# Products of the identity in PE's waits: two and four at a norm, ten at the double norm, twenty in the routing

## The chip, the cores and the metric

The kernel runs on one core of one Trainium2 chip. The metric is the device time of one execution, in microseconds, as the median of several runs. Everything is computed in float32. TensorE (PE in the rows) multiplies, VectorE (DVE) and ScalarE (ACT) do the elementwise work, SyncE (SP) issues nearly all weight loads, and GpSimd (POOL) makes a few copies.

## What is computed

One sequence of 256 tokens, 1024 channels, goes through a first block of two layers (RWKV-7 and latent attention beside each other, then a dense feed-forward layer in layer 0, a mixture of eight experts in layer 1) and a second block of two hybrid attention layers with feed-forward layers. Every half of a layer begins with an RMS norm:

```
def rmsnorm(x, g):
    y = x * rsqrt(mean(x * x, axis=-1, keepdims=True) + eps)
    return y * g

# first block, layers l = 0, 1
h = rmsnorm(x, norm_mix[l]) * (1 + scale) + shift        # "n1"
x = x + gate * (merged @ w_o[l])
h = rmsnorm(x, norm_ffn[l]) * (1 + scale) + shift        # "n2"
f = swiglu(h, ...) if l == 0 else moe_swiglu(h, ...)      # the experts: logits, top 2 of 8, softmax
x = x + gate * f
# between the blocks: rmsnorm(x, norm_final) is "nf", and the norm after it "m1" of layer 0
# second block, layers l = 0, 1
h = rms_norm(x, attn_norm[l])                             # "m1"
h = rms_norm(x, ffn_norm[l])                              # "m2"
x = x + (silu(gate) * up) @ w_ffn_out
```

## The kernel before

Activations lie transposed, channels on the 128 partitions and the 256 tokens along the free side, in eight tiles of 128 x 256. PE's program is written out by hand in one order (`def _(pe)`), and so are the programs of the other engines; semaphores are the only tie between them. Every product goes through the helper `mm` at L524, so nearly all PE rows carry that line. One float32 product is two records of the trace (one transpose is one record).

**Banks.** PE writes into four banks in rotation. `take(key)` gives the next bank and waits until its last reader has released it (`drained`); `take_upper` and `take_beside` do the same for other areas, which the rows call accum. Each call of `take` therefore moves all later uses of the rotation by one bank.

**A norm** has these steps on PE: sums over the channels, by products with one moving column (`zeroed_columns`, then `column_sums`, 12 records where single, 24 otherwise); then ACT takes the root of two columns and DVE the reciprocal, for which PE waits (`inverted`); then `norm_rows` spreads the result over 128 partitions with two products of 128 columns (four records, out<-con,ncol); then DVE multiplies x by it, tile after tile (at n1 and n2 ACT adds a shift to each), and PE waits for the first tile (`h_ready`) before the first product of the next projection. `norm_sums` is called for n2 of both layers, n1 of layer 1, m2 of both layers, and m1 of layer 1; `two_norm_sums` does m1 of layer 0 and nf together, after the experts. The very first norm uses neither.

**The routing** is the start of `experts`. PE turns h to natural order (four times four transposes, L880), with the logits' transposition between the first and the second; then comes a small product for lambda; then PE waits until DVE has picked the two experts of each token (`selected`), and counts positions (`pos`, ten records of 8 columns). From these DVE works out which expert stands at which place (`place_ids`, L2185); SP waits for that before it issues the first expert weights (L2808). DVE goes on to build selection matrices (`grouped`); PE waits for them and gathers the tokens with products of 480 columns (`static`). Then come 168 pieces of expert weights of 2 MB each, in five buffers.

Of the kernel before, what the change touches and what calls it, by code (L numbers as in the profile page):

```python
# [27 lines left out]
P = 128  # L28
# [194 lines left out]
def build(nc, A, out):  # L223
    ctx = ExitStack()
    with ctx:
# [9 lines left out]
        con = sb("con", [P, NCONST])  # L235
# [120 lines left out]
        def reader_of(key):  # L356

            return drained[used_banks[key][0]]
# [25 lines left out]
        ident, blk = c("ident"), c("blk")  # L384
# [132 lines left out]
        def _(pe):  # L517
# [4 lines left out]
            def mm(o, lhsT, rhs, start=True, stop=True, last=False, skip=False):  # L522

                ins = nc.tensor.matmul(o, lhsT, rhs, start=start, stop=stop, skip_group_check=skip)  # L524
                if wide_release and not last:
                    ins.then_inc(wide_used[wide_release.pop(0)], 1)
                elif release and not last:
                    ins.then_inc(ring_used[release.pop(0)], 1)
                return ins

            def take(key):

                b, k, per = used_banks[key] = banks.next()
                if k or per:
                    pe.wait_ge(drained[b], count(k, per))
                return bank[b], filled[b]
# [75 lines left out]
            def attention(tag, q_of, k_of, v_of, rows, take_scores, beside=None):  # L612
# [23 lines left out]
                for hd in range(n):  # L636
# [8 lines left out]
                    if beside:  # L645
# [6 lines left out]
                    mm(t[rows(hd), P:T], v_of(hd, 1), pT[:, hd % 2, T:T + P], False, True, last=True,  # L652
                       skip=True).then_inc(f, 1)

            def first_norm_sums(tag):

                place = []

                def pair(p):
                    if p == 0:  # L660
                        place.extend(take(tag + (0,)))
                    t, f = place
                    pe.wait_ge(x_squared, next_of("x_squared"))
                    for k in (2 * p, 2 * p + 1):
                        ins = mm(t[:, 0:T], ones[:, :], sq[:, k, :], k == 0, k == KD - 1, last=k == KD - 1)
                    if p == 3:
                        ins.then_inc(f, 1)

                return pair

            def zeroed_columns(key, take=take):

                t, f = take(key)
                mm(t[:, 0:TT], zeros, con[:, 0:TT], True, False, skip=True)
                return t, f
# [6 lines left out]

            def norm_rows(key, at, take=take):

                pe.wait_ge(inverted, next_of("inverted"))
                t, f = take(key + ("rows",))
                for a in range(TT):
                    ins = mm(t[:, a * P:(a + 1) * P], ncol[:, at + a:at + a + 1].to_broadcast([P, P]), ident, last=True)
                ins.then_inc(f, 1)

            def norm_sums(tag, take=take, single=False):

                def pair(p):
                    if p < 3:
                        return
                    t, f = zeroed_columns(tag + (0,), take)
                    one_ = ones[:, 0:1]
                    if single:
                        pe.wait_ge(squares_added, next_of("squares_added"))
                        column_sums(t, 0, sq, one_)  # L700
                        pe.wait_ge(x_squared, next_of("x_squared", 4))
                        column_sums(t, 6, sq, one_)
                        pe.wait_ge(x_squared, next_of("x_squared"))
                    else:
                        pe.wait_ge(squares_added, next_of("squares_added"))
                        column_sums(t, 0, sq, one_)
                        column_sums(t, 1, sq, one_)
                        pe.wait_ge(x_squared, next_of("x_squared", 3))
                        column_sums(t, 4, sq, one_)
                        column_sums(t, 5, sq, one_)  # L710
                        pe.wait_ge(x_squared, next_of("x_squared"))
                        column_sums(t, 6, sq, one_)
                    column_sums(t, 7, sq, one_, True).then_inc(f, 1)
                    norm_rows(tag, 2, take)

                return pair

            def two_norm_sums():

                def pair(p):  # L720
                    if p < 3:
                        return
                    (t0, f0), (t1, f1) = zeroed_columns(("nf", 0)), zeroed_columns(("m1", 0, 0))
                    pe.wait_ge(x_squared, next_of("x_squared", 8))
                    for k in (6, 7, 0):
                        if k == 0:
                            pe.wait_ge(squares_added, next_of("squares_added"))
                        column_sums(t1, k, sq, c("eps", 0, 1))
                        ins = column_sums(t1, k, sqg, ones[:, 0:1], k == 0)
                    ins.then_inc(f1, 1)  # L730
                    for k in (6, 7, 0):
                        ins = column_sums(t0, k, sq, ones[:, 0:1], k == 0)
                    ins.then_inc(f0, 1)
                    norm_rows(("m1", 0), 2)
                    norm_rows(("nf",), 6)

                return pair
# [136 lines left out]
            def experts(norm):  # L874

                for a in range(TT):
                    for g in range(2):
                        t, f = take(("hnat", a, g))
                        for i in range(4):
                            ins = nc.tensor.transpose(t[:, i * P:(i + 1) * P], h[:, g * 4 + i, a * P:(a + 1) * P], ident)  # L880
                        ins.then_inc(f, 1)
                        if a == g == 0:
                            pe.wait_ge(*read_out(("logit_parts",)))
                            t, f = take(("logits",))
                            for b in range(TT):
                                ins = mm(t[:, 8 * b:8 * b + 8], logit_parts[:, b * P:(b + 1) * P], c("pick_q", 0, 8), last=True)
                            ins.then_inc(f, 1)
                pe.wait_ge(lam_prod, next_of("lam_prod"))
                t, f = take(("lam",))
                mm(t[:, 0:4], ones[0:64, :], small[0:64, 0:4], last=True).then_inc(f, 1)  # L890
                pe.wait_ge(selected, next_of("selected"))
                t, f = take(("pos",))
# [3 lines left out]
                mm(t[:, 16:24], ones[:, :], router["sel"](0), True, False, last=True)  # L896
                mm(t[:, 16:24], ones[:, :], router["sel"](1), False, True, last=True).then_inc(f, 1)
                pe.wait_ge(*read_out(("hnat", 1, 1)))
                pe.wait_ge(grouped, next_of("grouped"))
                for k in range(KD):  # L900
                    t, f = take(("static", k))
# [27 lines left out]
                for n, (kind, i, k) in enumerate(PIECES):  # L929
                    first, last = (k == 0, k == KD - 1) if kind != "d" else (k % 4 == 0, k % 4 == 3)  # L930
# [6 lines left out]
                    for j in range(NJ):  # L937
                        key = ("e" + kind, i, j) if kind != "d" else ("ed", i, k // 4, j)
# [8 lines left out]
                        for c4 in range(4):  # L947
# [5 lines left out]
                            ins = mm(o[r, 0:WAYS], tokens, weights(n, s), first, last, last=last and c4 == 3, skip=True)  # L953
# [14 lines left out]
                for m in range(KD):  # L968
# [3 lines left out]
                    ins = combine(m)  # L972
# [8 lines left out]
            t, f = take(("c",))  # L981
# [5 lines left out]
            for k in range(0, KD, 2):  # L987
                t, f = take(("xT", k))
                for i in range(2):
                    for a in range(TT):  # L990
                        ins = nc.tensor.transpose(t[:, i * T + a * P:i * T + a * P + P],
                                                  x_nat[:, a, (k + i) * P:(k + i + 1) * P], ident)
# [20 lines left out]
            for l in range(2):  # L1013
# [38 lines left out]
                i = 0  # L1052
                for _, n, ms in B1_PIECES:
                    s, w = piece(8, n)
                    for lo, M, at in ms:
                        t, f = take(("in", l, at))
# [98 lines left out]
                for ch in range(NCH):  # L1155
# [4 lines left out]
                    for name in ("X", "Y"):  # L1160
                        ts = [take((name, l, ch, par)) for par in range(2)]
                        for j in range(RJ):
                            for par, (t, f) in enumerate(ts):
                                r = slice(64 * par, 64 * par + 64)
                                if name == "X":
                                    ins = mm(t[rc, j * 64:j * 64 + 64], AT[r, j, tc], state[r, j, :], last=True)
                                else:
                                    ins = mm(t[r, j * 64:j * 64 + 64], state[r, j, :], RT[r, j, tc], last=True)
# [4 lines left out]
                    t, f = take(("U", l, ch))  # L1173
                    for hd in range(HEADS):
                        ins = mm(t[rc, hd * 64:hd * 64 + 64], Tt4[a][rc, (hd % 2) * 4 + hd // 2, :],
                                 xrhs[rc, hd * 64:hd * 64 + 64], last=True)
# [3 lines left out]
                    t, f = take(("S", l, ch))  # L1180
                    for hd in range(HEADS):
# [4 lines left out]
                        ins = mm(o, Kn[rc, a, hc], Vn[rc, a, hc], False, True, last=True, skip=True)  # L1186
# [6 lines left out]
                for a in range(TT):  # L1193
                    ts = [take(("yl", l, 2 * a + cp)) for cp in range(2)]
                    for hd in range(HEADS):
# [3 lines left out]
                        i = (hd % 2) * 4 + hd // 2  # L1199
                        for cp, rc in halves:  # L1200
                            mm(ts[cp][0][r, at], U[rc, a, hc], RB4[a][rc, i, :], True, False, last=True, skip=True)
                        for cp, rc in halves:
                            ins = mm(ts[cp][0][r, at], Vn[rc, a, hc], RK4[a][rc, i, :], False, True, last=True, skip=True)
# [30 lines left out]
                t, f = take(("krot", l))  # L1234
                mm(t[0:96, 0:T], c("rot96")[0:96, :], qa[0:96, 5, :], last=True).then_inc(f, 1)
                s, w = piece(2)
                for i in range(4):
                    t, f = take(("kn_", l, i))
                    for k in range(2):
                        for half in range(2):  # L1240
                            at = (2 * i + half) * P
                            ins = mm(t[64 * half:64 * half + 64, 0:T], w(k, at, at + 64), qa[:, 3 + k, :], k == 0, k == 1,
                                     last=k == 1, skip=True)
                    ins.then_inc(f, 1)
                for a in range(TT):
                    t, f = take(("vn_", l, a))
# [27 lines left out]
                else:  # L1274
                    pe.wait_ge(router_in, next_of("router_in", 32))
                    t, f = take(("logit_parts",))
                    for k in range(KD):
                        r = slice(STRIP * (k % 4), STRIP * (k % 4 + 1))
                        ins = mm(t[r, 0:T], rt[:, k * STRIP:(k + 1) * STRIP], normed_h(k), k < 4, k >= 4, last=True, skip=True)
# [5 lines left out]
            for l in range(2):  # L1285
# [68 lines left out]
                for _, n, kind in B2_PIECES:  # L1354
# [3 lines left out]
                    if kind == "nat":  # L1358
                        for a in range(TT):
                            t, f = take(("nat", l, nat, a))  # L1360
# [7 lines left out]
                    elif kind == "idx":  # L1368

                        t, f = take(("tr", l, 10))  # L1370
                        for k in range(KD):
                            for half in range(2):
                                ins = mm(t[64 * half:64 * half + 64, 0:T], w(k, 0, 64), h[:, k, :], k == 0, k == KD - 1,
                                         last=k == KD - 1, skip=True)
# [3 lines left out]
                        for a in range(TT):  # L1378
                            t, f = take(("iw", l, a))
# [1520 lines left out]
```

## Time and profile before

| | |
|---|---|
| median of 3 runs | 2949.95 us (2945.87 to 2951.54) |
| the profiled execution, its own time | 2941.82 us |
| its span, first to last instruction | 2940.2 us |
| mean granted TensorE clock | 0.984 |
| PE, ACT, DVE busy | 2833.6, 489.0, 722.7 us |
| DMA | 634.18 MB, mean 216 GB/s |

Read it so: PE is busy nearly all the time, so what counts is how long PE's own work takes and what it waits for. The granted clock is TensorE's share of full speed: 1.00 is 2.4 GHz and 0.50 is 1.2 GHz. A mean of 0.984 says that it stood at the lower level for some 3% of the span. A matmul's busy time is longer than its share of the pace, since matmuls overlap: the pace is read from the time that a row of several records takes.

### The profile page before, as it was taken

The page shows a single profiled execution, that of the slowest core. Times are in us where ns is not written, and L with a number is a line of the kernel's source. Part 1 is how long each engine was busy: PE and PEld are TensorE (multiplying, and loading weights), DVE is VectorE, ACT ScalarE, POOL GpSimd, SP SyncE. Part 2 cuts the span into 40 slices and gives each one's busy share as a digit, 9 for nine tenths or more (in the row PEclk, how much of TensorE's full clock was granted, in tenths as well). Part 3 has the DMA queues.
Part 4 walks back from the last instruction along what each step waited for, and adds up shares of the span by engine and source line. Part 5 has one row for each costly group of instructions (what it writes and reads, how often), then busy time and mean ns, then how long its engine had stood idle before and what let it go on. Part 6 is the DMA issues. An engine that isn't in the chain of part 4 may idle for free.

```text
span 2940.2 us, 49988 instructions
## 1 busy us (share of the span) xinstructions
PE 2833.6 (96%) x20416; PEld 1872.1 (64%) x20416; DVE 722.7 (25%) x1713; ACT 489.0 (17%) x1007; POOL 233.2 (8%) x410
## 2 busy tenths in 40 slices
PE   7999999999988999999999999999999999999999
PEld 5777788887867432322222222277888888878888
DVE  4422454434243101011101101135520002632000
ACT  3213210032232100000000000014420003350000
POOL 4000000000000122222222121200000000000000
PEclk9999999999998999999999999999999999999999
DMA  9562378732220999999999999933343434333442
GB/s 299 163 196 95 101 252 275 259 111 81 67 86 29 353 362 374 375 378 372 378 371 378 370 385 368 362 117 120 115 138 120 166 125 140 120 113 123 150 159 85
DMA packets 435572, 634.18 MB, mean 216 GB/s; under 512 B 29802, under 2 KB 244992, under 8 KB 435216
## 3 DMA queue, kind: packets, MB, share of 16 engines
q1 hardware_dynamic: 406544, 600.97, 59.1%
q10 hardware_dynamic: 26400, 28.76, 3.0%
q8 instruction: 162, 2.65, 0.4%
q0 software_dynamic: 2400, 1.26, 0.2%
q14 instruction: 66, 0.54, 0.1%
HBM read 629.82 MB, written 1.05 MB: 215 GB/s over the span
## 4 chain that ended last, share of the span: by engine, by line
PE 67%; SPq 23%; issue 6%; DVE 2%; ACT 1%; DMA 1%; ACTq 0%; DVEq 0%
PE bank L524 47%; SPq L2808 20%; PE accum L524 19%; SPq L2794 2%; DVE w L1920 1%; SPq L2735 1%; PE bank L643 1%; DMA ring<-in_ada_w_dram 0%; ACT L1430 0%; DMA ring<-in_moe_w_dram 0%; PE bank L1084 0%; ACT sh L1430 0%; PE bank L880 0%; DVE h L1926 0%; ACT h L1430 0%
## 5 line engine op out<-in xcount | busy, mean ns | idle before, releaser
L524 PE MATMUL bank<-h,ring 128*128 128x256 f32 (+1 forms) x3712 | 824.4, 384 | 11.0 <-ACT w L1430 5.0
L524 PEld LDWEIGHTS bank<-h,ring 128*128 128x128 f32 (+1 forms) x3712 | 703.8, 192 | 120.3 <-issue 17.3
L524 PE MATMUL bank<-w 64*64 64x64 f32 (+3 forms) x4146 | 283.5, 332 | 13.0 <-DVE w L1920 6.2
L524 PE MATMUL bank<-ring,w 128*32 (+1 forms) x1742 | 240.9, 592 | 0.0
L524 PEld LDWEIGHTS bank<-w 64*64 64x64 f32 (+2 forms) x4146 | 148.2, 131 | 144.9 <-issue 131.7
L524 PE MATMUL accum<-w,ring 128*128 128x256 f32 x1056 | 233.2, 379 | 0.0
L524 PE MATMUL bank<-w,ring 128*128 128x256 f32 x1024 | 226.7, 382 | 4.8 <-DVE w L1920 3.9
L524 PEld LDWEIGHTS accum<-w,ring 128*128 128x128 f32 x1056 | 200.5, 190 | 27.6 <-issue 0.4
L524 PEld LDWEIGHTS bank<-w,ring 128*128 128x128 f32 x1024 | 194.3, 191 | 33.1 <-DVE w L1920 5.5
L1920 DVE TENSOR_TENSOR w<-bank,w 128x256 f32<-128x256 f32 (+1 forms) x114 | 61.2, 537 | 532.3 <-ACT w L1430 524.3
L524 PEld LDWEIGHTS bank<-ring,w 128*32 128x32 f32 x1742 | 67.0, 110 | 160.4 <-issue 160.4
L1430 ACT ACTIVATE w<-bank 128x256 f32<-128x256 f32 (+3 forms) x127 | 56.1, 451 | 678.5 <-PE bank L524 672.5
L524 PE MATMUL accum<-h,ring 128*128 128x256 f32 (+1 forms) x704 | 162.9, 386 | 1.4 <-issue 1.3
L2868 POOL COPY sg<-ring 128x512 f32 x102 | 59.9, 617 | 1122.2 <-DMA ring<-in_moe_w_dram 1091.8
L524 PEld LDWEIGHTS accum<-h,ring 128*128 128x128 f32 (+1 forms) x704 | 130.4, 189 | 22.9 <-issue 3.5
L524 PE MATMUL accum<-ring,w 128*32 128x512 f32 (+1 forms) x1072 | 128.4, 597 | 3.9 <-DMA ring<-in_moe_w_dram 2.9
L524 PE MATMUL bank<-ring,h 128*32 (+3 forms) x880 | 130.7, 506 | 0.0
L1430 ACT ACTIVATE h<-accum 128x512 f32<-128x512 f32 x28 | 15.3, 595 | 673.0 <-PE accum L855 673.0
L524 PE MATMUL accum<-w 128*32 128x512 f32 (+5 forms) x944 | 120.7, 541 | 5.9 <-DMA w<-in_moe_w_dram 3.5
L1920 DVE TENSOR_TENSOR w<-accum,w 128x512 f32<-128x512 f32 x24 | 16.6, 692 | 443.6 <-PE accum L524 441.9
L524 PEld LDWEIGHTS bank<-ring,h 128*32 128x32 f32 (+1 forms) x880 | 73.9, 139 | 51.0 <-issue 44.7
L524 PEld LDWEIGHTS accum<-w 128*32 128x32 f32 (+2 forms) x944 | 40.8, 129 | 70.6 <-issue 42.8
(327 smaller groups left out, 2408.7 us busy)
## 6 DMA issues: line engine op xcount, KB each, us to landing
ring<-in_moe_w_dram SPq DMA_DIRECT2D x816, 256.0 KB, 7.7
w<-in_moe_w_dram SPq DMA_DIRECT2D x528, 256.0 KB, 7.6
ring<-in_w_in_dram SPq DMA_DIRECT2D x76, 1024.0 KB, 5.2
ring<-in_w_ffn_in_dram SPq DMA_DIRECT2D x44, 1024.0 KB, 5.2
ring<-in_ffn_w_dram SPq DMA_DIRECT2D x33, 1024.0 KB, 7.8
ring<-in_ada_w_dram SPq DMA_DIRECT2D x24, 1024.0 KB, 11.3
w<-in_ada_w_dram ACTq DMA_DIRECT2D x24, 1024.0 KB, 5.9
ring<-in_w_ffn_out_dram SPq DMA_DIRECT2D x22, 1024.0 KB, 4.8
```

The costliest lines, as they stand in the source:

```text
L524: ins = nc.tensor.matmul(o, lhsT, rhs, start=start, stop=stop, skip_group_check=skip)
L643: ins = nc.tensor.transpose(t[:, i * P:(i + 1) * P], p[:, i * P:(i + 1) * P], ident)
L1430: return nc.scalar.activation(o, i, f, **kw)
L1920: return V.tensor_tensor(o, a, b, op)
L2735: sp_.dma_start(ring[:, s, 0:kc * n].rearrange("p (c n) -> p c n", c=kc), src).then_inc(ring_loaded[s], 16)
L2794: expert = [sp_.value_load(place_ids[0:1, r:r + 1], min_val=0, max_val=EXPERTS - 1) for r in range(EXPERTS)]
L2808: sp_.dma_start(to[:, r * WAYS:(r + 1) * WAYS], src.rearrange("o p n -> p (o n)")).then_inc(wide_loaded[n % WIDE], 16)
L2868: ins = pool.tensor_copy(copies[n % 2][:, b, :], wide[n % WIDE][:, bass.ds(way[b] * WAYS, WAYS)])
```

## The change

A new helper `keep_busy(n)` takes the next bank and issues n products of the identity with the first 128 columns of the constants (128 x 128, float32, two records each). Nothing reads the result; the last product releases the bank itself. It is called

- with 2 in `norm_rows`, before the wait for `inverted`, so at every norm of `norm_sums` and twice in `two_norm_sums`;
- after `norm_rows` in `norm_sums`, before the wait for `h_ready`: with 4 for n1 and n2, with 2 for m1 and m2;
- with 10 in `two_norm_sums`, before the wait for the squares of x;
- with 20 in `experts`, after `pos`, before the wait for `grouped`.

```
+            warm = [0]
+
+            def keep_busy(n):
+
+                key = ("warm", warm[0])
+                warm[0] += 1
+                t, f = take(key)
+                for i in range(n):
+                    ins = mm(t[:, 0:P], ident, con[:, 0:P], last=i in (0, n - 1))
+                    if i == 0:
+                        ins.then_inc(f, 1)
+                ins.then_inc(reader_of(key), 1)
+
             def norm_rows(key, at, take=take):
 
+                keep_busy(2)
                 pe.wait_ge(inverted, next_of("inverted"))
...
                     norm_rows(tag, 2, take)
+                    keep_busy(4 if tag[0] in ("n1", "n2") else 2)
...
                     (t0, f0), (t1, f1) = zeroed_columns(("nf", 0)), zeroed_columns(("m1", 0, 0))
+                    keep_busy(10)
                     pe.wait_ge(x_squared, next_of("x_squared", 8))
...
                 pe.wait_ge(*read_out(("hnat", 1, 1)))
+                keep_busy(20)
                 pe.wait_ge(grouped, next_of("grouped"))
```

No other engine's program changes. In the orders below a product counts once, so x2 is four records.

PE at n2 of layer 0, before: sums, rows, then the feed-forward layer's first products.

```order
475 L524 MATMUL accum<-con,cpad 128x2
476 L524 MATMUL accum<-ones,h 128x1 x6
477 L524 MATMUL accum<-con,ncol 128x128 x2
478 L524 MATMUL bank2<-h,ring 128x256 x16
479 L524 MATMUL bank3<-h,ring 128x256 x16
```

And now:

```order
475 L524 MATMUL accum<-con,cpad 128x2
476 L524 MATMUL accum<-ones,h 128x1 x6
477 L524 MATMUL bank2<-con 128x128 x2
478 L524 MATMUL accum<-con,ncol 128x128 x2
479 L524 MATMUL bank3<-con 128x128 x4
480 L524 MATMUL bank0<-h,ring 128x256 x16
481 L524 MATMUL bank1<-h,ring 128x256 x16
```

The new products stand on both sides of the rows, and the next products lie two banks further on.

PE at the double norm, before; nf's sums go to bank1, m1's to bank2, the two norms' rows to bank3 (m1) and bank0 (nf).

```order
2085 L524 MATMUL bank1<-con,cpad 128x2
2086 L524 MATMUL bank2<-con,cpad 128x2
2087 L524 MATMUL bank2<-con,h 128x1 x2
2088 L524 MATMUL bank2<-ones,sg 128x1 x2
...
2093 L524 MATMUL bank1<-ones,h 128x1 x6
2094 L524 MATMUL bank3<-con,ncol 128x128 x2
2095 L524 MATMUL bank0<-con,ncol 128x128 x2
2096 L524 MATMUL bank1<-h,ring 128x256 x8
```

And now:

```order
2092 L524 MATMUL bank0<-con,cpad 128x2
2093 L524 MATMUL bank1<-con,cpad 128x2
2094 L524 MATMUL bank2<-con 128x128 x10
2095 L524 MATMUL bank1<-con,h 128x1 x2
...
2101 L524 MATMUL bank0<-ones,h 128x1 x6
2102 L524 MATMUL bank3<-con 128x128 x2
2103 L524 MATMUL bank0<-con,ncol 128x128 x2
2104 L524 MATMUL bank1<-con 128x128 x2
2105 L524 MATMUL bank2<-con,ncol 128x128 x2
2106 L524 MATMUL bank3<-h,ring 128x256 x8
2107 L524 MATMUL bank0<-h,ring 128x256 x8
```

Here m1's rows now go to bank0, in which nf's sums lie, where before they had a free bank; and the second product tile after them goes to that bank too.

PE in the routing, before:

```order
977 L524 MATMUL bank3<-small,ones 128x4
978 L524 MATMUL bank0<-sg,con 128x8 x2
979 L524 MATMUL bank0<-sg,ones 128x8 x3
980 L524 MATMUL bank1<-sh,sg 128x480 x2
981 L524 MATMUL bank2<-sh,sg 128x480 x2
```

And now:

```order
983 L524 MATMUL bank1<-small,ones 128x4
984 L524 MATMUL bank2<-sg,con 128x8 x2
985 L524 MATMUL bank2<-sg,ones 128x8 x3
986 L524 MATMUL bank3<-con 128x128 x20
987 L524 MATMUL bank0<-sh,sg 128x480 x2
```

Forty records now stand between the positions and the gathering of the tokens.

## Rows read from the trace of the kernel before

**Rows 1.** The page: busy times, and the granted clock in 40 slices.

```profile
PE 2833.6 (96%) x20416; PEld 1872.1 (64%) x20416; DVE 722.7 (25%) x1713; ACT 489.0 (17%) x1007; POOL 233.2 (8%) x410
PEclk9999999999998999999999999999999999999999
```

**Rows 2.** Stretches around n2 of layer 0, PE alone; columns in the first row.

```profile
core 0: us, PE busy (x), PEclk, DMA share, GB/s
373.50:377.80 4.30, 2.54 (x19) 1.00 0.67 216
378.90:382.20 3.30, 3.30 (x10) 0.50 0.00 0
382.30:385.60 3.30, 3.30 (x17) 1.00 0.00 0
```

**Rows 3.** The same view at n1 (two), m2 of layer 0, m1 of layer 1.

```profile
617.80:620.80 3.00, 1.23 (x4) 0.50 0.58 203
620.90:624.60 3.70, 3.70 (x9) 0.50 0.00 0
...
2205.40:2208.40 3.00, 2.97 (x7) 0.50 0.29 101
...
2443.90:2447.30 3.40, 3.40 (x10) 0.50 0.02 5
```

**Rows 4.** Timeline of n2, layer 0: start, us, work, idle before and its releaser.

```profile
373.69 1.65 PE L524 MATMUL accum<-ones,h 128*128 128x1 f32 x12
...
375.96 0.71 PE L524 MATMUL accum<-con,ncol 128*128 128x128 f32 x4 [0.62 <-DVE ncol L1940]
...
377.88 1.52 PE L524 MATMUL bank<-h,ring 128*128 128x256 f32 x5 [1.21 <-ACT h L1430]
```

**Rows 5.** Timeline: sixteen transposes of 128 columns at full clock.

```profile
113.01 1.97 PE L1084 MATMUL bank<-con,w 128*128 128x128 f32 x16
```

**Rows 6.** A stretch that holds nothing but products of four columns.

```profile
1959.30:1962.50 3.20, 3.20 (x31) 1.00 0.43 143
```

**Rows 7.** Groups by form of the stretch of rows 6.

```profile
L524 PE MATMUL bank<-ring,h 128*128 128x4 f32 x31 | 3.6, 253 | 0.0
```

**Rows 8.** Two stretches of the double norm, then one behind that of rows 6.

```profile
1942.20:1947.60 5.40, 5.40 (x26) 0.50 0.00 0
1947.70:1948.90 1.20, 1.20 (x4) 0.50 0.00 0
...
1962.70:1966.00 3.30, 3.30 (x9) 0.50 0.35 80
```

**Rows 9.** Timeline of the double norm.

```profile
1940.03 0.61 PE L524 MATMUL bank<-con,h 128*128 128x1 f32 x4 [2.53 <-ACT sg L1430]
...
1943.24 2.70 PE L524 MATMUL bank<-ones,h 128*128 128x1 f32 x12
...
1945.80 2.06 PE L524 MATMUL bank<-con,ncol 128*128 128x128 f32 x8
...
1947.67 0.77 PE L524 MATMUL bank<-h,ring 128*128 128x256 f32 x1
```

**Rows 10.** Two stretches of the routing.

```profile
943.40:950.60 7.20, 7.20 (x33) 0.50 0.00 0
...
955.60:959.10 3.50, 3.50 (x5) 0.50 0.04 5
```

**Rows 11.** Timeline of the routing.

```profile
945.11 2.80 PE L880 MATMUL bank<-con,h 128*128 128x128 f32 x12
...
950.77 0.17 DVE L1926 SCALAR_TENSOR_TENSOR sg<-bank,con 128x8 f32<-128x8 f32 x1 [3.53 <-PE bank L524]
...
955.59 1.14 PE L524 MATMUL bank<-sh,sg 128*128 128x480 f32 x1 [4.93 <-issue]
```

**Rows 12.** SP's waits from 1010 to 1060: us in total, times, longest.

```profile
SPq L2808 <- PE accum L524: 7.7, 5, 3.1
```

**Rows 13.** A stretch of the experts.

```profile
1000.00:1050.00 50.00, 49.75 (x452) 1.00 1.02 365
```

## The prediction

> **What bounds the kernel now.** I read the page first: PE is busy for 96% of the span, and the granted clock shows a few nines among full slices [rows 1]. So the time is PE's own work, and apart from its waits the only thing that stretches this work is the lower clock. Then I asked for the granted clock in stretches, to find where it is low. Behind each norm that the change touches, and in the routing, it stands at 0.50 for a few microseconds. The reader is to see in [rows 2] that 3.3 us at 0.50 hold ten records of the feed-forward layer where the next 3.3 us at 1.00 hold 17, and that the stretch just before holds 19 records but only 2.54 us of busy time. In [rows 3] the same stands at n1 of layer 1 (low from 617.8 to 624.6), m2 and m1; m2 of layer 1 looks like m2 of layer 0. The double norm is low from 1942.2 to 1948.9 [rows 8, 9], the routing from 943.4 at the latest to 959.1 [rows 10]. PE is the chain at all of these places but one: among the experts the DMA engines are full (share 1.02 [rows 13]), and what counts there is when their stream starts.
>
> **What makes the clock fall.** Before n2's low stretch PE did twelve products of one column, waited 0.62 us, spread the rows with four records and waited 1.21 us [rows 4]. It was hardly ever idle, but streamed almost nothing. The sharper case is [rows 6, 7]: PE busy 3.20 of 3.20 us, all with products of four columns, and right behind it the clock is 0.50 [rows 8]. So instructions don't hold the clock here; columns do. The change adds products of 128 columns, each record as wide as those of the rows. That is the right kind of work.
>
> The Trainium skill says otherwise on this point: TensorE: Matmul & The Clock Gate, section "Why this matters for your kernels", names idle gaps of PE between bursts of matmuls as what brings the clock down. By that rule the short gaps at n2 would be harmless, and filling them would bring nothing; what time that gives is rival (d). The trace does not agree: the clock fell behind the stretch of [rows 6], which has no gap at all.
>
> **What a product costs.** Sixteen records of 128 columns take 1.97 us at full clock [rows 5], (1.97 - 0.27) / 15 = 0.11 us each, with 0.27 us as the length of the last. Twelve at the low clock take 2.80 us [rows 11], (2.80 - 0.42) / 11 = 0.22. A product is two records: two products cost 0.45 us, four 0.9, ten 2.2, twenty 4.4 us at full clock, twice that at the low one. They stand ahead of waits of 0.62, 1.21, 2.53 and 4.93 us [rows 4, 9, 11]. The last product before a wait began 0.25 us before the idle time does, so there is a little more room than the idle figure. At full clock all fit, and cost nothing. If the cover were gone, all 64 of them (6 at n1 and at each n2, 4 at m1 and at each m2, 14 at the double norm, 20 in the routing) would cost 14 us.
>
> **Norm by norm.** A low stretch costs half of that part of it in which PE is the chain.
>
> n2 of layer 0: 3.4 us low, all in products [rows 2]: 1.7 us. In the 4.2 us from the sums to the first product the change puts twelve records (1.3 us of streaming) beside the four of the rows (0.45). I take it that the fall goes: 1.7 us.
>
> n1 of layer 1: 3.8 us of products and the four row records, 1.23 us [rows 3] instead of 0.71 [rows 4]: 1.9 + 0.5 = 2.4 us. But the fall came at 617.8, at the end of 24 sums of one column (2.8 us), before any new product could act. Only the second half of the stretch goes for certain; in other executions the whole may go or hardly anything. Bounds 0 and 2.4, I take 1.5.
>
> m2, twice: 3.0 us low in products [rows 3], 1.5 us each. There the change adds eight records, not twelve, and in executions whose clock did not fall there is nothing to win. I take 1.2 each. m1 of layer 1: 3.4 us low [rows 3], 1.7 us; 24 sums as at n1, so again only part: 1.2.
>
> **The double norm.** From 1942.2 to 1947.6, 26 records run at 0.22 instead of 0.11 us, 2.5 us more, and the low clock goes on into products for 1.2 us, 0.6 more [rows 8, 9]: 3.1 us. The ten products fill 2.2 of the 2.53 us of waiting. But behind them 36 sums of one column follow, 4 us with nothing wide, and nothing is added among them: I expect a shorter low stretch, later, which still costs about 1 us. And there is a new wait: m1's rows now go to the bank that holds nf's sums, so they need ACT to have read them, where before they followed the last sum at once (1945.80, no idle in the row). Nearest row: the whole way from the last sum over ACT and DVE is 0.62 us of idleness [rows 4]; the new wait is a part of that, on top of the 0.45 us of the two products. Bounds 0.45 and 0.9, I take 0.55, nearer to the products, which are sure. 3.1 - 1.0 - 0.55 = 1.5 us.
>
> **The routing.** From 943.4 to 950.6, 33 records at the low clock keep PE from the positions, and DVE waits 3.53 us for them [rows 10, 11]. At full clock the transposes take 1.4 us less, the ten positions 1.0 less, the logits ahead of them 0.5: about 2.9 us earlier for `place_ids`, and so for the stream of expert weights. The products that lie between here and n2 (router columns, paced by ACT) are narrow, so I expect the clock to fall later rather than not at all: bounds 0 and 2.9, I take 1.0. The twenty products fill 4.4 of 4.93 us. At the low clock they would take 8.8; since they themselves bring the clock back on the way, I expect 6 to 7, so the gathering starts 1 to 2 us late. It then runs at full clock, where now it loses 3.5 / 2 = 1.75 us up to 959.1 [rows 10]. These cancel. Behind it the transfers hide what is left, as SP waits for PE only 7.7 us in all [rows 12].
>
> **The sum.** 1.7 + 1.5 + 1.2 + 1.2 + 1.2 + 1.5 + 1.0 = 9.3 us. The profiled execution took 2941.8, so the same execution would take 2932.5. It stood 8.1 us under the median of the runs, though it shows a low stretch at every one of these places; that offset is not in what changes. On the median: 2949.95 - 9.3 = 2940.6.
>
> **Rivals.**
>
> (a) The clock falls anyway, later. Two or four products are too little beside the narrow sums, and the low stretch only moves from the wait into the products behind it, where it costs its full half. For it: n1's fall came before the place of the new products. Against it: twelve wide records at n2 are three times the four that stood there. Then only the double norm and half of n2, n1 and routing remain, about 1.5 + 2.5 = 4 us: 2946.
> (b) Everything holds: 1.7 + 2.4 + 1.5 + 1.5 + 1.7 + 2.5 + 2.9 = 14.2 us: 2935.7. Against it are the narrow sums and the router's products.
> (c) Slower. The mechanism is the twenty products at the low clock: 8.8 us against 4.93, 3.9 us late into the gathering, and SP waits for PE at 1010 to 1060 [rows 12], so PE's lateness can reach the end. With the new wait of 0.55 and no gain at the norms: 2954.4. It decides if the clock has not come back some 3 us after 950.6, and if nothing is won before.
>
> (d) Only long idleness counts, not narrow work. Then the gaps of 0.62 and 1.21 us at a single norm are no cause, filling them brings nothing, and only the places with waits of 2.53 and 4.93 us [rows 9, 11] gain: 1.5 + 1.0 = 2.5 us, 2947.4. [rows 6] speaks against it.
>
> **How the numbers follow.** Forecast, with gains of 6 to 12 us: 0.59. (a) 0.20, (b) 0.12, (c) 0.05, (d) 0.04. The range reaches from all of (b) to most of (a): 2935 to 2949. A measurement of this kernel can tell about 0.2%, 5.9 us, from no change. Faster by more: the forecast and (b), 0.71. Within: (a), (d) and most of (c), 0.26. Slower by more needs (c) and a further 1.5 us of loss: 0.03.
>
> **What the profile of the changed kernel would show.** At n2, 1.00 through to the products, with 17 records per 3.3 us; at m2 the same; at n1, m1 and the double norm at most one short low stretch each. The rows' idle time falls from 0.62 to about 0.2 us while ACT and DVE start no later. At the double norm, m1's rows 0.5 us or more behind the last sum. DVE's wait for the positions under 3 us. It is wrong if 0.50 stands behind n2 and both m2, or if `static` starts over 3 us behind `grouped`.

## The result and the profile after

The changed kernel takes 2931.98 us (median of 5, 2929.87 to 2935.34) where the kernel before takes 2949.74 (median of 5): the ratio is 0.9943, with an interval of 0.9933 to 0.9954. That is 17.8 us faster on the medians, against 9.3 forecast, and below the range, which began at 2935. Run once more (below), it gave 0.9927 (0.9915 to 0.9938). The direction was right, the size too small by nearly a factor of two.

The two profiled executions differ by less, 2932.7 against 2940.2 us of span. The first view after, its core with span and mean clock:

```profile
core 0: 2932.7 us, clock 0.987
```

And the page's clock slices:

```profile
PEclk9999999999999999999999999999999999999999
```

The one eight among the slices of [rows 1], the routing, is gone. The same stretches as in [rows 2, 3, 8, 10], PE alone (stretch, its length, busy time and records, granted clock, DMA share, GB/s):

```profile
374.10:378.40 4.30, 3.92 (x31) 1.00 0.65 200
378.50:381.80 3.30, 3.30 (x16) 1.00 0.14 46
616.20:622.90 6.70, 6.70 (x26) 0.50 0.36 126
623.00:626.60 3.60, 3.60 (x18) 1.00 0.00 0
2199.10:2202.10 3.00, 2.90 (x14) 1.00 0.37 122
2449.20:2455.80 6.60, 6.60 (x20) 0.50 0.44 126
939.00:946.20 7.20, 6.83 (x57) 1.00 0.01 2
948.70:952.20 3.50, 3.50 (x9) 1.00 0.03 4
1933.80:1940.40 6.60, 6.60 (x32) 0.50 0.00 0
```

Read it against before. At n2 of layer 0 the stretch ahead of the products now has 31 records instead of 19, and the products run at 1.00, 16 in 3.3 us where [rows 2] have ten. m2 is at full clock as well. The routing is too, in both its stretches, where [rows 10] stood at 0.50. But n1 is low for 6.7 us as before, and the double norm for 6.6 us.

Near m1 of layer 1 the low stretch no longer lies where [rows 3] have it (2449.20 above). Behind m1 come the projections (64 records of 256 columns), then the index weights (32 records of 4 columns, as those of [rows 6, 7]), then further products. Before:

```profile
2443.28 12.44 PE L524 MATMUL bank<-h,ring 128*128 128x256 f32 x64 [0.66 <-DVE h L1926]
2455.64 3.74 PE L524 MATMUL bank<-ring,h 128*128 128x4 f32 x32
2459.24 3.70 PE L524 MATMUL bank<-h,ring 128*128 128x256 f32 x16
```

And now:

```profile
2435.58 10.75 PE L524 MATMUL bank<-h,ring 128*128 128x256 f32 x64 [0.22 <-DVE h L1943]
2446.26 4.44 PE L524 MATMUL bank<-ring,h 128*128 128x4 f32 x32
2450.56 6.34 PE L524 MATMUL bank<-h,ring 128*128 128x256 f32 x16
```

The projections are 1.7 us shorter, at full clock. But the clock then falls among the index weights' records, and the sixteen records behind them take 6.34 us instead of 3.70. The same happens behind the double norm, where 3.4 us of low clock [rows 8] became 6.8, from 1954.2 on. The prediction has no term for these two places, and wrote that m1 and the double norm would show at most one short low stretch each.

The timeline of n2 shows that the products cost nothing there (columns as in [rows 4]):

```profile
375.75 0.69 PE L524 MATMUL bank<-con 128*128 128x128 f32 x4
...
376.51 0.71 PE L524 MATMUL accum<-con,ncol 128*128 128x128 f32 x4
377.06 1.06 PE L524 MATMUL bank<-con 128*128 128x128 f32 x8
...
378.43 0.45 PE L524 MATMUL bank<-h,ring 128*128 128x256 f32 x1 [0.31 <-ACT h L1447]
```

The rows begin as soon as DVE's reciprocal is there, and 0.31 us of the second wait are still free. From the rows to the first product pass 1.92 us, as in [rows 4].

In the routing:

```profile
940.28 1.51 PE L896 MATMUL bank<-con,h 128*128 128x128 f32 x12
...
943.80 4.52 PE L524 MATMUL bank<-con 128*128 128x128 f32 x39
943.87 0.17 DVE L1943 SCALAR_TENSOR_TENSOR sg<-bank,con 128x8 f32<-128x8 f32 x1 [1.45 <-PE bank L524]
...
948.64 0.67 PE L524 MATMUL bank<-sh,sg 128*128 128x480 f32 x1 [0.32 <-DVE sh L1937]
```

The twelve transposes take 1.51 instead of 2.80 us, and DVE waits 1.45 us for the positions instead of 3.53 [rows 11]. The twenty products fit: 39 of their records take 4.52 us (0.11 each, as forecast), and the gathering still waits 0.32 us for DVE.

### The profile page after: what moved, and what is told of

Same layout as the page of the kernel before. It is cut to its first block, busy times and chain, and to the rows that moved or that the text cites. A ratio compares the mean times of both kernels' runs of the same rounds, so it can differ in the third digit from the quotient of the medians.

```text
span 2932.7 us, 50245 instructions
## 1 busy us (share of the span) xinstructions
PE 2844.6 (97%) x20544; PEld 1883.8 (64%) x20544; DVE 722.9 (25%) x1713; ACT 488.5 (17%) x1007; POOL 232.3 (8%) x410
## 4 chain that ended last, share of the span: by engine, by line
PE 69%; SPq 22%; issue 6%; DVE 2%; ACT 1%; DMA 1%; ACTq 0%; DVEq 0%
PE bank L524 48%; PE accum L524 20%; SPq L2825 19%; SPq L2811 2%; DVE w L1937 1%; SPq L2752 1%; PE bank L643 1%; DMA ring<-in_ada_w_dram 0%; ACT L1447 0%; PE bank L1101 0%; DMA ring<-in_moe_w_dram 0%; ACT sh L1447 0%; PE accum L871 0%; ACT w L1538 0%; DVE w L1940 0%
## 5 line engine op out<-in xcount | busy, mean ns | idle before, releaser
L524 PEld LDWEIGHTS bank<-h,ring 128*128 128x128 f32 (+1 forms) x3712 | 702.1, 191 | 115.8 <-issue 13.6
L524 PEld LDWEIGHTS accum<-h,ring 128*128 128x128 f32 (+1 forms) x704 | 130.3, 189 | 21.4 <-issue 2.1
L1447 ACT ACTIVATE h<-accum 128x512 f32<-128x512 f32 x28 | 15.3, 595 | 673.3 <-PE accum L871 673.3
```

Source lines behind the costliest of these rows:

```text
L1447: return nc.scalar.activation(o, i, f, **kw)
```

## The experiments

To compare places I use two measures. One is the time from the last record of 256 columns ahead of a norm to the 60th such record behind its reciprocal, worked out from each trace (in the routing: to the end of the 32 gathering records). At m1 and the double norm it goes to the 90th, which lies behind the index weights' products of four columns. The work in between is the same in every kernel, but for the products added. The other is the mean granted clock of every single execution. An execution of the kernel before has 0.980 to 0.985, its profiled one 0.984.

Each of the first group ran against the kernel before on the same chip.

**The kernel before, once more.** No edit.

> The kernel before, unchanged. The change brought 17.8 us on the medians but only 7.5 us between the two profiled spans. Theory A (the profiled execution of before was a light one): another execution shows more low clock than 94 us-equivalents (mean under 0.984) and a span near 2948. Theory B (timed and profiled executions differ by something else, as the transfers): the clock is 0.984 again and the time near 2949.7 all the same. Ratio 1.000 to the kernel before.

Ratio 1.000 (0.999 to 1.001). Its profiled execution took 11.3 us longer than the one that I had predicted from:

```profile
die 0 (median of its cores): 2951.5 us, clock 0.983
```

Up to the first expert weights the two traces differ by 1.2 us and show low clock at the same places (96.9 us of it in the whole of the one span, 100.4 in the other). The difference arises among the experts: from SP's first issue to the last landing 952.9 us in one, 961.5 in the other. So both theories have a part: the execution was light in low clock by a little (12 executions of this run have a mean clock of 0.9821), and lucky in the experts' transfers by up to 9 us. The gap of 7.5 us between the profiled spans of before and after is therefore too small a measure of the change.

**Only the twenty products in the routing.**

```
-                keep_busy(2)
...
-                    keep_busy(4 if tag[0] in ("n1", "n2") else 2)
...
-                    keep_busy(10)
```

> Only the twenty products in the routing; no others. Theory A (the clock at n2 and through the routing brings the weights' stream forward): the twenty alone come too late for place_ids, which stays where it was; the gathering starts up to 2 us late and runs at full clock. Gain 0 to 2 us. Rival B (the twenty are what wins in the routing, since PE reaches the first pieces sooner and SP waits less for it): 3 to 5 us.

Ratio 0.9981 (0.9970 to 0.9992), 5.6 us: above what my theory A allowed. In its trace the positions were reached at full clock, without any product ahead of them, so the fall at n2 of layer 1 does not come in every execution; it stood in four of five without wide products there (the five are this one, the kernel before twice, and the kernels with only the double norm's products and with narrow products, below). What the twenty do behind the positions:

```profile
951.11 4.71 PE L524 MATMUL bank<-con 128*128 128x128 f32 x40
956.15 6.30 PE L524 MATMUL bank<-sh,sg 128*128 128x480 f32 x15 [0.33 <-DVE sh L1934]
```

PE reached the first expert piece 12.8 us behind SP's first issue, where the kernel before needs 14.5.

**Only the two and four at the norms.**

```
-                    keep_busy(10)
...
-                keep_busy(20)
```

> The two and four products at all norms, without the ten and the twenty. Theory A: these carry most of the gain, 12 to 15 of 17.8 us, of which some 3 us are an earlier place_ids after n2 of layer 1. Theory B: the long waits carry it, and these bring at most 6 us.

Ratio 0.9954 (0.9940 to 0.9968), 13.6 us. Theory A holds. `place_ids` is written 12.3 us behind n2's reciprocal instead of 15.3, and SP issues the first expert weights 3.0 us earlier too. But in the routing's idle time the clock fell after all, and the gathering paid (stretches as above):

```profile
938.00:946.00 8.00, 5.23 (x38) 1.00 0.00 0
947.00:953.50 6.50, 4.96 (x7) 0.50 0.22 66
```

The norms' and the routing's part, 13.6 + 5.6 = 19.2 us, are together what the whole change gives (16.8 and 21.6 us in its two measurements).

**The same products, four columns wide.**

```
-                    ins = mm(t[:, 0:P], ident, con[:, 0:P], last=i in (0, n - 1))
+                    ins = mm(t[:, 0:4], ident, con[:, 0:4], last=i in (0, n - 1))
```

> All 64 products as in the change, in the same places and banks, but with 4 columns instead of 128 (weights unchanged, so PE issues as many records in nearly the same time). If columns hold the clock, it falls as before the change at every place and the time is that of before, +0 to +2 us (the new wait at the double norm). If PE's mere activity, the weight loads or the new bank order make the gain, the time is that of the change, 17.8 us faster.

The clock is that of before, 0.9822 in the mean of 12 executions. At n2 and in the routing:

```profile
375.00:377.40 2.40, 1.94 (x16) 1.00 0.99 326
378.40:381.70 3.30, 3.30 (x10) 0.50 0.00 1
951.00:958.50 7.50, 7.50 (x37) 0.50 0.01 3
```

PE was busy all the time with the 37 narrow records and the clock stayed low, so they took nearly twice as long, and the gathering began 3.4 us later than in the kernel before, counted from n2's reciprocal. It is the columns that hold the clock here, not the instructions and not the weight loads. Yet the ratio is 0.9983 (0.9971 to 0.9994), 5 us faster than before and not 0 to 2 slower, as I expected. The interval comes close to 1, but the mean clock does not explain the step. Its profiled execution was one of its slowest (span 2953.1 us). What makes these 5 us is left open, and a part of the change's own gain may have the same cause. The new bank order is a candidate, since this kernel shares it with the change; no run takes the banks without issuing products.

**The change, once more.** No edit. This and the next three ran on one chip.

> The changed kernel, unchanged, a second time. Theory A (the gain is low clock that goes, at half its length, and an earlier stream of expert weights; the profile of before was light in both): mean clock 0.987 to 0.989 against 0.980 to 0.985 of before, ratio 0.994 as first, and the experts' stream from first issue to last landing somewhere between 951 and 962 us, by chance. Theory B (the change shortens the stream itself by some 9 us): the stream is again 951, where before has 961.

Ratio 0.9927 (0.9915 to 0.9938), 2934.5 us beside 2956.4.

```profile
die 0 (median of its cores): 2935.6 us, clock 0.989
```

Its stream of expert weights took 956.0 us, the first time 951.1: theory A, the stream varies. n1 was at full clock here, where the first execution had 6.8 us of low clock. The six executions have a mean clock of 0.9883, the 17 of before 0.9816. If PE were the chain all through its low clock, that would be 0.0067 x 2950 = 20 of the 22 us. That is an upper estimate: a straight line through clock and time of the kernel before, on each of three chips (29, 17 and 17 executions), gives 1.8 to 1.9 us for a step of 0.001, not 2.95, and by that slope it is 12 to 13 us.

**Wide sums, with no product added.** The one moving column of the norms' sums is repeated 128 times, the product that zeroes their place grows from 2 columns to 256 with it, and the index weights' product takes 68 columns instead of 4. As many records as before.

```
-                mm(t[:, 0:TT], zeros, con[:, 0:TT], True, False, skip=True)
+                mm(t[:, 0:TT * P], zeros, con[:, 0:TT * P], True, False, skip=True)
...
-                    ins = mm(t[:, a:a + 1], src[:, k, a * P:(a + 1) * P], by, False, final, last=final, skip=True)
+                    ins = mm(t[:, a * P:(a + 1) * P], src[:, k, a * P:(a + 1) * P], by.to_broadcast([P, P]), False, final, last=final,
+                             skip=True)
...
-                            contract(t[:, 0:4], KD, lambda k: h[:, k, a * P:(a + 1) * P],
-                                     lambda k: w(k, 64, 68)).then_inc(f, 1)
+                            contract(t[:, 0:68], KD, lambda k: h[:, k, a * P:(a + 1) * P],
+                                     lambda k: w(k, 0, 68)).then_inc(f, 1)
```

(and ACT reads column 0 of each 128, or columns 64 to 67, accordingly).

> The kernel before, with no product added. Only the moving side of the norms' column sums is 128 columns wide instead of one (the same column repeated), and 68 instead of 4 in the index weights. As many records, at nearly the same pace, as the weight load bounds them. If columns hold the clock: the falls behind sums shrink without any added instruction, low clock falls from 103 to about 70 us, gain 10 to 15 us. If it is idleness that counts: nothing changes, ratio 1.000.

Ratio 0.9940 (0.9927 to 0.9952), mean clock 0.9903: 17.7 us from wider operands alone, more than the 10 to 15 expected. Twelve sums at n2, timeline, and the products behind, stretch:

```profile
374.34 1.50 PE L524 MATMUL accum<-ones,h 128*128 128x128 f32 x12
```

```profile
378.40:381.70 3.30, 3.30 (x16) 1.00 0.22 76
```

128 columns cost no more time than one: twelve records take 1.50 us where [rows 4] have 1.65. Only the zeroing product costs something, as the sums begin 0.3 us later. This is the sharpest test of what the clock follows, since the number of instructions is that of before and the waits are not filled. How much of it is the sums' and how much the index weights', no run separates. The fall behind the index weights, at least, is in none of the four kernels in which they are wide.

**The change and the wide sums together.** Both edits.

> The change and the wide sums together. If columns hold the clock, the falls that the change left (n1 6.8 us, double norm 6.8, behind the double norm 6.8, m1 6.8 us of low clock) go: another 20 to 27 us of low clock, 8 to 12 us faster than the change, about 2921 where before has 2950. If not, the time of the change.

Ratio 0.9911 (0.9898 to 0.9925), 2929.6 us beside 2934.5 of the change alone and 2956.4 of before. In its trace none of the seven places has any low clock:

```profile
614.00:622.00 8.00, 7.51 (x53) 1.00 0.41 131
936.00:946.00 10.00, 9.14 (x62) 1.00 0.00 0
...
2432.00:2440.00 8.00, 7.61 (x41) 1.00 0.27 93
```

The step beyond the change is 5 us, not the 8 to 12 that I expected: the mean clock is 0.9906 against 0.9883, a step of 0.0023. Some falls of the change don't occur in every execution, so there was less to win.

**Only n2 of layer 1 and the routing.** Of the change, the six products at n2 of layer 1 and the twenty.

```
-                keep_busy(2)
+                if key == ("n2", 1):
+                    keep_busy(2)
...
-                    keep_busy(4 if tag[0] in ("n1", "n2") else 2)
+                    if tag == ("n2", 1):
+                        keep_busy(4)
...
-                    keep_busy(10)
```

> Only the six products at n2 of layer 1 and the twenty in the routing. Theory A (the six keep the clock through the router's narrow products, the twenty up to the pieces; together 20 us of low clock, 3.0 us earlier place_ids and 4.8 us earlier pieces): ratio 0.9975 or so, 5 to 8 us. My prediction's term said 1.0 us (then the ratio is 0.9997), so this run tells whether that term is the one mis-sized.

Ratio 0.9978 (0.9968 to 0.9988), 6.5 us (3.5 to 9.5). The prediction had 1.0 us for all of this. The place takes 29.85 us instead of 34.65. How the 6.5 us divide between the six and the twenty these runs don't show: the twenty alone gave 5.6.

The last four ran on one chip.

**Only the double norm's products.**

```
-                keep_busy(2)
+                if key[0] == "nf" or key == ("m1", 0):
+                    keep_busy(2)
...
-                    keep_busy(4 if tag[0] in ("n1", "n2") else 2)
...
-                keep_busy(20)
```

> Only the double norm's products: ten before the squares, two before each of its two rows; nothing elsewhere. My prediction's term: 1.5 us gained. Rival (from the traces so far, in which the place took 36.95 and 35.33 us with the change and 34.49 to 36.16 without): nothing is gained or up to 1 us lost, as the low clock only moves behind the sums and m1's rows wait for ACT. Then the ratio is 1.000 to 1.001.

Ratio 0.9996 (0.9987 to 1.0005): nothing. The rival was right.

```profile
1939.11 2.48 PE L524 MATMUL bank<-con 128*128 128x128 f32 x20
1941.79 0.61 PE L524 MATMUL bank<-con,h 128*128 128x1 f32 x4 [0.19 <-ACT sg L1446]
...
1944.49 1.76 PE L524 MATMUL bank<-ones,h 128*128 128x1 f32 x12
1946.11 1.20 PE L524 MATMUL bank<-con 128*128 128x128 f32 x4
1947.10 1.06 PE L524 MATMUL bank<-con,ncol 128*128 128x128 f32 x4
1947.95 1.06 PE L524 MATMUL bank<-con 128*128 128x128 f32 x4
```

The ten fill the wait. Then 4.4 us of one-column sums follow, and the clock falls in them:

```profile
1941.80:1945.40 3.60, 3.60 (x33) 1.00 0.00 0
1945.50:1948.90 3.40, 3.40 (x18) 0.50 0.00 0
1962.70:1969.30 6.60, 6.60 (x21) 0.50 0.39 118
```

The products ahead of the rows then run at the low clock (four records in 1.20 us) and delay m1's rows by 1 us. The low stretch is still only half as long as the 6.8 us of [rows 8, 9]. But behind the index weights (the third line), it is 6.8 us long where the kernel before had 3.4, and the sum is the same.

**The change without the double norm's products.**

```
-                keep_busy(2)
+                if key[0] != "nf" and key != ("m1", 0):
+                    keep_busy(2)
...
-                    keep_busy(10)
```

> The change without the double norm's fourteen products. If they bring nothing, the ratio is that of the change, 0.993 to 0.994, or 0.5 us better; if they bring 1.5 us, it is 0.0005 worse, which this measurement hardly sees; the place itself in the trace tells: 34.5 to 36.2 us as before, and m1's rows right behind the last sum.

Ratio 0.9945 (0.9929 to 0.9960), as the change's. The place took 37.60 us here, with 13.7 us of low clock, more than the 34.5 to 36.2 I named. Together with the run before it, the double norm's products bring nothing that can be seen.

**The change and the wide sums, without the double norm's products.** The edit of the last run on top of the wide sums.

> The change and the wide sums, without the double norm's products. There the change's products had 2.5 us of idleness to fill, which the wide sums don't. If the ten still hold the clock there, this is 1 to 2 us slower than with them (2929.6 beside 2956.4 of before), and low clock stands in the double norm; if the wide sums are enough, it is 0.5 us faster, as the wait on nf's bank is gone.

Ratio 0.9920 (0.9906 to 0.9934), beside 0.9911 with them: the intervals overlap. In the trace 3.4 us of low clock stand at the double norm, which had none with the products, and the place takes 0.9 us longer. That speaks for the ten once the sums behind them are wide; it is one execution of each.

**The wide sums and the twenty only.** No product at any norm.

> The wide sums and of the change the twenty only; no product at any norm. If the wide sums are enough at the norms, this equals the change with the wide sums (ratio 0.991), except that the router's narrow products come later at low clock (3 us at place_ids). If the two and four are needed beside them, 3 to 6 us slower than that (0.992 to 0.993).

Ratio 0.9937 (0.9924 to 0.9951), 2929.4 us beside 2924.5 of the run just above: the two and four at the norms still bring 5 us beside wide sums. In its trace n2 and n1 have 3.4 us of low clock each.

## Why the prediction was wrong

The mechanism was right. Columns hold the clock (rival (d), idleness, is refuted by the narrow products and by the wide sums), the products fit their waits, and no engine was delayed, but for the rows at the double norm. The sum was mis-sized, by its terms. Places as mean over executions without and with the products of that place (in brackets how many; kernels with only a part of a place's products, narrow ones or wide sums are left out), in us:

| place | without | with | gain | forecast |
|---|---|---|---|---|
| n2, layer 0 | 19.16 (5) | 17.58 (4) | 1.6 | 1.7 |
| n1, layer 1 | 21.27 (5) | 19.86 (4) | 1.4 | 1.5 |
| n2, layer 1, and routing | 34.61 (3) | 29.85 (4) | 4.8 | 1.0 |
| double norm | 35.77 (5) | 35.86 (3) | -0.1 | 1.5 |
| m2, layer 0 | 18.81 (5) | 16.97 (4) | 1.8 | 1.2 |
| m1, layer 1 | 29.41 (5) | 29.70 (4) | -0.3 | 1.2 |
| m2, layer 1 | 19.07 (5) | 16.97 (4) | 2.1 | 1.2 |
| sum | | | 11.3 | 9.3 |

**The routing is the step that failed**: its term was 1.0 us, and its products, with the six of n2 ahead of it, measured 6.5 us by themselves. Two parts of it were wrong. I took 1.0 of the 2.9 us for `place_ids`, expecting that the router's products would bring the clock down anyway, as they are narrow. They are narrow on the weights' side alone, 32 columns of the array; each streams 256 moving columns, as this row of the kernel before shows:

```profile
939.80 3.76 PE L524 MATMUL bank<-h,rt 128*32 128x256 f32 x16 [1.21 <-ACT h L1430]
```

In all five executions with the six products the clock was full from there to the positions, and `place_ids` came 3.0 us earlier; the bound was the right value. (Without them it was full in one of five, so on average the six are worth somewhat less.) And I wrote that the twenty products' lateness and the faster gathering "cancel" and that behind it "the transfers hide what is left". The twenty were not late, as the clock was already full when they began; the gathering took 1.7 us less; and with the twenty alone the whole kernel gained 5.6 us, so it was not all hidden.

By which way that reaches the end is not shown. SP's waits for PE among the experts are a candidate. Here they are from 960 to 1800 us (us in total, times, longest) for five kernels: the kernel before, once more; the norms only; the twenty only; the change, once more; the narrow products.

```profile
SPq L2808 <- PE accum L524: 9.1, 7, 3.1
```

```profile
SPq L2823 <- PE accum L524: 11.2, 8, 3.1
```

```profile
SPq L2822 <- PE accum L524: 5.9, 5, 3.1
```

```profile
SPq L2825 <- PE accum L524: 6.0, 5, 2.1
```

```profile
SPq L2825 <- PE accum L524: 14.0, 9, 2.6
```

The stream took 957.9 us in the mean of five executions without the twenty and 954.0 in eight with them, each spread over some 9 us. Within each group that was measured together the difference has the same sign, 2 to 4 us. So the twenty may shorten it by some 3 us. But the narrow products had the longest waits of all, and their stream took 957.3 us, less than the 960.0 and 961.4 of the two executions without the twenty on the same chip. So the waits alone don't explain the stream.

**Double norm and m1** were forecast at 1.5 and 1.2, and measured nothing. What failed is a term that the sum does not have: the index weights' products of four columns behind both, the very records of [rows 6], with the fall of [rows 8] behind them. Up to the 60th record of 256 columns, ahead of the index weights, the two places did gain, 2.2 us at the double norm (23.6 without, 21.4 with) and 2.0 at m1 (17.6 and 15.7). From there to the 90th they lost 2.3 us each, as the low clock there went from 3.4 us or none, in most executions, to 6.8. This is rival (a), a fall that moves, at these two places alone. With the index weights widened it went away: m1 takes 26.8 us, not 29.7. At the double norm the two products ahead of m1's rows, which ran at the low clock, cost up to 1 us besides, where the bounds of 0.45 to 0.9 us had been worked out for full clock; no wait on nf's bank shows beside them.

The two m2 won more than forecast. None of their ten executions without the products had a full clock, for which I had taken something off, and in three of the ten the low stretch was 6.8 us, not 3.4.

**The base.** 11.3 us at the places and perhaps 3 in the stream make 14, within the interval of the first measurement (13.6 to 19.8 us) but under its middle and under that of the second (18.3 to 25.1). Two things that I took for fixed were not. I set every price by one execution of before, whose clock of 0.984 lies at the upper side of the 0.980 to 0.985 that its executions have; and I saw that it stood 8.1 us under the median and called that offset irrelevant. How much of the gain is low clock depends on the reckoning: 20 of 22 us at half the length of all low clock, 12 to 13 by the slope within the kernel before. The first can't be exact, as by it the wide sums would bring 26 us, and they brought 17.7. With the second, the 5 us of unexplained gain in the run with narrow products fit the rest, but no run shows that they are the same. That much stays open.

The range failed because its lower end was the sum of the highest prices from that one execution. Rival (b) reached 2935.7 with all falls gone; the change reached 2932 with three of them left. That the terms of the double norm, m1 and the routing erred in opposite directions, so that the sum of the places missed by only 2 us, was luck.

## What to carry to other kernels

When PE's clock falls, count how many columns it streams there, not how many instructions it issues or how long it idles; and before any product is added to fill a wait, widen the narrow products that are there already, here up to 128 columns, since that costs next to nothing (it brought 17.7 us by itself, and 26 us of 2956 together with the change). Look past the place too: a fall that is prevented behind a norm can come at the next narrow stretch, so that stretch needs a term of its own. Place the clock's price where its stretch leads: the low clock in the routing, ahead of a long stream, was worth 6.5 us where a norm's was worth 1.4 to 2.1. And take the price from the spread of several executions' clocks, since one profiled execution can be 8 us away from the median.

## What the runs showed of the hardware

- A float32 record with 128 x 128 weights takes 0.11 to 0.12 us at full clock with 1, 4, 68 or 128 columns: 12 records of 128 columns in 1.50 us, 12 of one column in 1.65, 32 of 4 columns in 3.74, 32 of 68 in 3.79. With 256 columns it takes 0.17 us (64 in 10.75).
- 37 records of four columns, back to back for 7.5 us, left the clock at 1.2 GHz; forty of 128 columns in the same place stood at 2.4.
- The same falls don't come in every execution: n1 had 6.8, 3.4, 3.4 and 0 us of low clock in four executions with the change's products there.
- The transfer of the 352 MB of expert weights took 949.6 to 961.5 us from first issue to last landing in the fourteen profiled executions, a spread wider than the gain of several of the edits.
